# First norm of a layer kernel: raw tiles turned as they land, its weights at the copies from PSUM, its roots at later copies

## The reference, cut to what matters

```python
def rmsnorm(x, g):
    xf = x.astype(jnp.float32)
    y = xf * lax.rsqrt(jnp.mean(xf * xf, axis=-1, keepdims=True) + EPS)
    return (y * g.astype(jnp.float32)).astype(x.dtype)

def layer_forward(x, pos0, lw, pool_prev, rgc_prev, rgh0, sc_prev, nsa_fn):
    h = rmsnorm(x, lw['norm_mix_g'])
    proj = jnp.einsum('bld,dn->bln', h, lw['w_in'])
    pu, rx, rgate, q, kv, ng, sc = split_cols(proj, SPLIT_SIZES)
    ...
    x = x + jnp.einsum('blm,md->bld', y, lw['w_out'])
    x = x + moe_ffn(rmsnorm(x, lw['norm_ffn_g']), ...)
```

## Time and profile before

| | us |
|---|---|
| median of 3 runs | 881.01 |
| lowest, highest | 880.95, 881.67 |
| the profiled execution | 879.65 |
| its span in the trace | 877.9 |
| PE busy, PE weight load | 743.2, 387.7 |
| DVE, ACT, POOL busy | 212.1, 143.0, 188.5 |
| first instruction of PE | 13.67 after the span's start |
| first projection (A0) starts | 20.3 |
| experts begin | about 390 |

### The profile page before, as it was taken

How to read it: one execution, slowest core, us unless ns; L and a number is a source line. 1 busy time by engine, 2 the same in 40 slices (tenths; PEclk the granted TensorE clock), 3 DMA queues, 4 the chain that set the end, 5 groups by cost and what they waited for, 6 DMA issues and landing times.

```text
span 877.9 us, 10180 instructions
## 1 busy us (share of the span) xinstructions
PE 743.2 (85%) x3636; PEld 387.7 (44%) x3636; DVE 212.1 (24%) x571; ACT 143.0 (16%) x348; POOL 188.5 (21%) x188
## 2 busy tenths in 40 slices
PE   3999999979898999949999997878787778777883
PEld 3788788867766645533333332222222222222220
DVE  4231103275849511561011101010010010100110
ACT  4212313104152521110101000000000000000000
POOL 7010000070300000011332331322313213223121
PEclk9999999989987999969999999999999999999997
DMA  9651733020340099249999999999999999999992
GB/s 312 120 150 61 240 132 103 2 74 1 121 168 1 4 395 418 100 160 371 411 411 408 409 410 409 415 406 418 406 416 413 408 412 417 408 416 409 414 416 88
DMA packets 77013, 247.04 MB, mean 281 GB/s; under 512 B 24952, under 2 KB 44303, under 8 KB 52363
## 3 DMA queue, kind: packets, MB, share of 16 engines
q1 hardware_dynamic: 63825, 231.48, 66.8%
q0 software_dynamic: 11776, 8.58, 4.4%
q10 hardware_dynamic: 1378, 6.54, 1.9%
HBM read 240.47 MB, written 24.92 MB: 302 GB/s over the span
## 4 chain that ended last, share of the span: by engine, by line
PE 40%; SPq 32%; DMA 12%; DVE 9%; issue 4%; ACT 2%; POOL 0%; ACTq 0%; POOLq 0%; DVEq 0%
PE bank L1090 36%; SPq L579 22%; SPq L586 10%; DMA reg_b<-in_exp_w_gu 6%; PE bank L1093 3%; DMA reg_a<-in_exp_w_gu 3%; DMA ffn_in<-reg_x 1%; DMA reg_x<-in_x_prompt 1%; DVE reg_a L1758 1%; DVE reg_a L1838 1%; DVE reg_y L2048 1%; DVE reg_a L1748 1%; DVE reg_x L1748 0%; DVE small L1799 0%; ACT reg_y L1073 0%
## 5 line engine op out<-in xcount | busy, mean ns | idle before, releaser
L1090 PE MATMUL bank<-reg_w,reg_y 128*64 128x512 f32 (+2 forms) x512 | 138.5, 586 | 16.9 <-DMA reg_w<-in_exp_w_gu 16.8
L1090 PE MATMUL bank<-reg_a,reg_y 128*64 128x512 f32 x528 | 124.2, 606 | 22.3 <-DMA reg_a<-in_exp_w_gu 16.6
L1090 PE MATMUL bank<-reg_b,reg_y 128*64 128x512 f32 x528 | 122.6, 599 | 20.8 <-DMA reg_b<-in_exp_w_gu 15.1
L2052 DVE TENSOR_TENSOR reg_y<-reg_y,bank 128x256 f32<-128x256 f32 x32 | 13.5, 421 | 418.7 <-ACT reg_y L1073 418.7
L1090 PEld LDWEIGHTS bank<-reg_w,reg_y 128*64 128x64 f32 (+2 forms) x512 | 45.5, 146 | 98.3 <-issue 55.5
L1090 PE MATMUL bank<-reg_b,reg_w 128*128 128x260 f32 x384 | 85.3, 383 | 0.0
L1090 PEld LDWEIGHTS bank<-reg_a,reg_y 128*64 128x64 f32 x528 | 34.7, 138 | 103.2 <-issue 51.1
L1090 PEld LDWEIGHTS bank<-reg_b,reg_y 128*64 128x64 f32 x528 | 34.8, 136 | 99.5 <-issue 56.9
L1090 PEld LDWEIGHTS bank<-reg_b,reg_w 128*128 128x128 f32 x384 | 72.7, 190 | 12.1 <-issue 1.1
L684 POOL TENSOR_TENSOR small<-small 128x1 f32<-128x1 f32 (+4 forms) x18 | 20.4, 1137 | 200.2 <-DVE small L1887 71.2
L754 POOL DMA_INDIRECT out_y_p<-reg_y,reg_h x16 | 25.3, 1582 | 167.2 <-ACT reg_y L1077 167.2
(11 more groups left out here) (340 smaller groups left out, 645.0 us busy)
## 6 DMA issues: line engine op xcount, KB each, us to landing
reg_a<-in_exp_w_gu SPq DMA_DIRECT2D x44, 1024.0 KB, 27.6
reg_b<-in_exp_w_gu SPq DMA_DIRECT2D x44, 1024.0 KB, 28.1
reg_w<-in_exp_w_gu SPq DMA_DIRECT2D x40, 1024.0 KB, 28.0
reg_a<-in_exp_w_down SPq DMA_DIRECT2D x22, 1024.0 KB
reg_b<-in_exp_w_down SPq DMA_DIRECT2D x22, 1024.0 KB, 28.0
reg_h<-in_exp_w_down SPq DMA_DIRECT2D x20, 1024.0 KB
reg_w<-in_w_in SPq DMA_DIRECT2D x9, 1024.0 KB, 10.7
reg_w<-in_w_out SPq DMA_DIRECT2D x2, 2048.0 KB, 10.5
```

What stands on the lines that cost most here:

```text
L1090: return eng.matmul(out, lhsT, rhs, start=start, stop=stop, skip_group_check=True)
L2052: tt(hid[b], silu[b], bank[2 + b][:, 256:512], ALU.mult).then_inc(S["hid_made"], 1)
```

## The change

The weights of the norm are loaded as 8 rows of 128 (4 KB) and turned by PE into `gain_col`, a column per chunk of channels; DVE copies it. PE turns the raw `x_in` tiles, each as soon as its load is there, not `xn`. The copies out of PSUM multiply by `gain_col`: ACT in four activations of 128 columns with a scale for each `xTa`, DVE in one multiply for each `xTb`. ACT's squares stand between these copies. The sample tile still gets its root before it is turned (`xn`, now last in PE's order: bank `xT4`), and its weights at the copy. The roots of tiles 0 to 3 are multiplied in twice: in `kv_rows` as the scale of ACT's copies, which wait for all five roots; and for the features, by a new job `RS`: DVE makes four diagonal matrices from the roots (`root_diag`), PE multiplies them by `ones` after the last projection, so that each partition holds all 512 roots, and DVE multiplies `xnT` (8 x 512 columns) in place by that bank. PE waits for it ahead of `features("U")`. One semaphore of the expert stage is counted on another one, to save a semaphore.

```diff
@@ psum_jobs
-    take("xT4")
+    take("gain")
     for i in range(4):
         take(f"xTa{i}")
         take(f"xTb{i}")
+    take("xT4")
...
+    take("RS")
     take("K3")
     take("R3")
@@ SP
-            eng.dma_start(gain_mix, a["norm_mix_g"].rearrange("l d -> (l d)").partition_broadcast(128)).then_inc(S["gain_loaded"], 16)
+            eng.dma_start(gain_rows, a["norm_mix_g"].rearrange("l (c p) -> (l c) p", p=128)).then_inc(S["gain_loaded"], 16)
@@ ACT
-            for i in TILES:
+            def square_tile(i):
                 eng.wait_ge(x_loaded[i], 16)
                 eng.activation(xn[0:ROWS[i], i, :], x_in[0:ROWS[i], i, :], ACT.Square, accum_out=sumsq[0:ROWS[i], i:i + 1]).then_inc(S["xsq_done"], 1)
-            ps = taken(eng, "xT4")
-            copied(copy(xnT[:, :, SEQ:T], ps[:, 0:64].rearrange("p (c t) -> p c t", c=8)), "xT4")
+            square_tile(4)
+            drained(eng, "gain")
             for i in range(4):
                 ps = taken(eng, f"xTa{i}")
-                copied(copy(xnT[:, 0:4, COL[i]:COL[i] + 128], ps[:, :].rearrange("p (c t) -> p c t", c=4)), f"xTa{i}")
+                for c in range(4):
+                    ins = eng.activation(xnT[:, c, COL[i]:COL[i] + 128], ps[:, 128 * c:128 * c + 128], ACT.Copy, scale=gain_col[:, c:c + 1])
+                copied(ins, f"xTa{i}")
+                square_tile(i)
...
                 ps = taken(eng, f"A{i}")
+                eng.wait_ge(S["rstd_made"], NTILE)
+                root = rstd[0:r, i:i + 1]
...
-                copy(qn_buf[n % 2][0:r, 0:256], ps[0:r, 0:256])
-                copied(copy(rows[0:r, i, 0:256], ps[0:r, 256:512]), f"A{i}")
+                eng.activation(qn_buf[n % 2][0:r, 0:256], ps[0:r, 0:256], ACT.Copy, scale=root)
+                copied(eng.activation(rows[0:r, i, 0:256], ps[0:r, 256:512], ACT.Copy, scale=root), f"A{i}")
...
-                copy(gates[0:r, i, :], ps[0:r, 256:W_LAST])
-                copied(copy(win[0:r, i, :], ps[0:r, 0:256]), f"C{i}")
+                eng.activation(gates[0:r, i, :], ps[0:r, 256:W_LAST], ACT.Copy, scale=root)
+                copied(eng.activation(win[0:r, i, :], ps[0:r, 0:256], ACT.Copy, scale=root), f"C{i}")
@@ PE
+            eng.wait_ge(S["gain_loaded"], 16)
+            filled(turn(claim(eng, "gain")[:, 0:KC], gain_rows), "gain")
+            for i in range(4):
+                eng.wait_ge(x_loaded[i], 16)
+                for k, name in enumerate(("xTa", "xTb")):
+                    ps = claim(eng, f"{name}{i}")
+                    for c in range(4):
+                        ins = turn(ps[:, 128 * c:128 * c + 128], x_in[:, i, 512 * k + 128 * c:512 * k + 128 * c + 128])
+                    filled(ins, f"{name}{i}")
             eng.wait_ge(S["xn_made"], 1)
             ps = claim(eng, "xT4")
...
+            eng.wait_ge(S["root_spread"], 1)
+            ps = claim(eng, "RS")
+            for i in range(4):
+                ins = mm(ps[:, 128 * i:128 * i + 128], ones, root_diag[:, i, :], True, True)
+            filled(ins, "RS")
             turn_qk(4)
...
+            drained(eng, "RS")
             features("U")
@@ DVE
+            def ask_root(n):
+                r = ROWS[TILES[n]]
                 eng.wait_ge(S["xsq_done"], n + 1)
+                ts(sumsq[0:r, TILES[n]:TILES[n] + 1], sumsq[0:r, TILES[n]:TILES[n] + 1], 1.0 / D, EPS, ALU.mult, ALU.add).then_inc(S["rstd_asked"], 1)
+            ps = taken(eng, "gain")
+            copied(eng.tensor_copy(gain_col, ps[:, 0:KC]), "gain")
+            ask_root(0)
+            drained(eng, "gain")
             for i in range(4):
                 ps = taken(eng, f"xTb{i}")
-                copied(eng.tensor_copy(xnT[:, 4:8, COL[i]:COL[i] + 128], ps[:, :].rearrange("p (c t) -> p c t", c=4)), f"xTb{i}")
+                copied(tt(xnT[:, 4:8, COL[i]:COL[i] + 128], ps[:, :].rearrange("p (c t) -> p c t", c=4), gain_col[:, 4:8].unsqueeze(2).to_broadcast([128, 4, 128]), ALU.mult), f"xTb{i}")
+                ask_root(i + 1)
+                if i == 1:
+                    eng.wait_ge(S["rstd_made"], 1)
+                    ts(xn[0:NS, 4, :], x_in[0:NS, 4, :], rstd[0:NS, 4:5], None, ALU.mult).then_inc(S["xn_made"], 1)
+            ps = taken(eng, "xT4")
+            copied(tt(xnT[:, :, SEQ:T], ps[:, 0:64].rearrange("p (c t) -> p c t", c=8), gain_col.unsqueeze(2).to_broadcast([128, KC, NS]), ALU.mult), "xT4")
+            eng.wait_ge(S["rstd_made"], NTILE)
+            for i in range(4):
+                ins = ts(root_diag[:, i, :], ident, rstd[:, i:i + 1], None, ALU.mult)
+            ins.then_inc(S["root_spread"], 1)
...
+            ps = taken(eng, "RS")
+            copied(tt(xnT[:, :, 0:SEQ], xnT[:, :, 0:SEQ], ps[:, :].unsqueeze(1).to_broadcast([128, KC, SEQ]), ALU.mult), "RS")
             eng.wait_ge(S["gates_tanh"], 1)
```

More of the change, by code:

```diff
@@ L214, in layer_kernel @@
         reg_q = Region("reg_q", 2080)
-        small = Region("small", 2399)
+        small = Region("small", 2407)
         gu_w = [r.t[:, 0:8192].rearrange("p (c n) -> p c n", c=8) for r in (reg_a, reg_b, reg_w)]
@@ L234, in layer_kernel @@
         raw = reg_x.t[:, :].rearrange("p (c t) -> p c t", c=2)
-        gain_mix = reg_y.cut(D)
+        gain_rows = reg_y.cut(128)[0:KC]
+        root_diag = reg_y.cut(512, "p (t n) -> p t n", t=4)
         par_rows = reg_y.cut(128)[0:P_ROWS]
@@ L367, in layer_kernel @@
         x1_sq = small.cut(10, "p (t h) -> p t h", t=5)
+        gain_col = small.cut(KC)
         gain_x = small.cut(8, "p (s c) -> p s c", s=2)
@@ L408, in layer_kernel @@
             vcache_loaded consts_made vector_chain pool_chain
[L409 removed]
+            xsq_done rstd_asked rstd_made xn_made root_spread hss_made hrs_made qk_normed gates_tanh gates_raw
             rows_stored states_stored params_made sp_exp_asked sp_exp sample_scores q_masked_made
@@ L810, in kv_rows @@
                     return
-                copy(qn_buf[n % 2][0:r, 0:256], ps[0:r, 0:256])
-                copied(copy(rows[0:r, i, 0:256], ps[0:r, 256:512]), f"A{i}")
+                eng.activation(qn_buf[n % 2][0:r, 0:256], ps[0:r, 0:256], ACT.Copy, scale=root)
+                copied(eng.activation(rows[0:r, i, 0:256], ps[0:r, 256:512], ACT.Copy, scale=root), f"A{i}")
                 ps = taken(eng, f"B{i}")
-                copied(copy(rows[0:r, i, 256:512], ps[0:r, 0:256]), f"B{i}")
+                copied(eng.activation(rows[0:r, i, 256:512], ps[0:r, 0:256], ACT.Copy, scale=root), f"B{i}")
                 ps = taken(eng, f"C{i}")
-                copy(gates[0:r, i, :], ps[0:r, 256:W_LAST])
-                copied(copy(win[0:r, i, :], ps[0:r, 0:256]), f"C{i}")
+                eng.activation(gates[0:r, i, :], ps[0:r, 256:W_LAST], ACT.Copy, scale=root)
+                copied(eng.activation(win[0:r, i, :], ps[0:r, 0:256], ACT.Copy, scale=root), f"C{i}")
             def feature_qk(i):
@@ L1101, in _ @@
             filled(ins, "xT4")
-            for i in range(4):
-                eng.wait_ge(S["xn_made"], i + 2)
-                for k, name in enumerate(("xTa", "xTb")):
-                    ps = claim(eng, f"{name}{i}")
-                    for c in range(4):
-                        ins = turn(ps[:, 128 * c:128 * c + 128], xn[:, i, 512 * k + 128 * c:512 * k + 128 * c + 128])
-                    filled(ins, f"{name}{i}")
             def project_samples():
@@ L1481, in turn_tokens @@
                 eng.wait_ge(x_gathered[b], gathered)
-                eng.sem_inc(S["xe_arrived"], 1)
+                eng.sem_inc(S["gather_asked"], 1)
                 by_channel = xe_rows[b].rearrange("n (p c) -> n c p", c=4)
```

11 lines of the change are left out of this document (1 added, 10 removed).

## The result

The changed kernel takes 874.59 us (median of 5, 871.75 to 875.90) against 881.39 (880.95 to 882.01) of the kernel before in the same comparison: ratio 0.9925, interval 0.991 to 0.994. The profiled execution took 875.42, its span is 873.7 (before: 879.65 and 877.9). The forecast was 876.4, within 874.0 to 878.9: the sign holds, and the time lies in the range, near its lower end. By the medians the gain is 6.8 us where 4.6 was forecast; by the two profiled executions it is 4.2.

The account below looks back on a forecast made before the run. PE's chain from the first projection (A0) was taken to bound the kernel, so A0's gain reaches the end: 7.1 - 0.2 - 0.9 - 1.4 = 4.6 us off the 881.01 median, giving 876.4, range 874.0 to 878.9.

Parts of the forecast that it names:

- The pass: DVE's in-place multiply of 4096 feature columns by the roots in `RS`'s bank: 4.47 us, expected within 4.2 to 4.8.
- The stall: PE waits at sample 7's second half, which gets `RS`'s bank: 4.47 + 0.1 - 3.15 = 1.4 us, bounds 0 and 3.0.
- rival B: At sample 7's second half: DVE's pass ends within its cover, no stall, 1.4 us better, 875.0; chance 0.12.
- rival E: DVE's pass runs at a third of the rate, 13.4 us; PE stands 10.3 and the kernel is slower, 885.3; chance 0.03.
- `RS` on PE: Four matmuls of 128 columns after the last projection, 0.88 us, wholly on the path.
- The gap: PE's wait before tile 0's turned queries: 1.2 us instead of 0.97, as ACT's last copies are scaled; 0.2 lost.
- Rival D: Something not starting with PE sets a later time and swallows the gain, giving 879.5 to 881; chance 0.07.
- the loads: Prompt tiles and weight chunks all land one tile's time, 1.28 us, earlier: tile 0 at 5.85, first chunk at 12.7.
- what A0 waits for: The first projection waits for the sample tile, scaled by 12.55, then small turns; starts at 13.4, 7.1 us earlier.
- Rival C: Before A0: all turns at the clock's low level, rising 2 us into A0; tile 0 1.5 later, 877.9; chance 0.16.
- Roots: POOL's powers, 0.54 us each or 5.10 if held; last at 17.0 or 21.6, ACT needs it at 20.4; no cost.
- The sum: Whole kernel: 7.1 at A0 - 0.2 gap - 0.9 `RS` matmuls - 1.4 stall = 4.6 us gained.

Follow-up runs that it names:

- e4_spread_kept: The changed kernel with the norm weights' 512 KB spread load put back ahead of the prompt tiles, read by nobody; 876.39 us, ratio 0.9956.
- e2_rs_late: The changed kernel with `RS` one stage later: matmuls after sample 7's work, DVE's pass behind the gates' instructions; 873.52 us, ratio 0.9926.
- g1_rs_late: The edit of e2_rs_late to the changed kernel, run once more beside the unedited changed kernel; 875.07 us, ratio 0.9933.
- g2_after: The changed kernel unedited, run as the partner of g1_rs_late; 874.49 us, ratio 0.9938.
- e3_no_rs: The changed kernel without `RS`: no matmuls with ones, no DVE pass, so the features lack their roots; 874.41 us, ratio 0.9935.
- f4_half_first: The changed kernel with `RS` late, the first weight chunk loaded between tiles 1 and 2 and its half of A0 done there; 874.84 us, ratio 0.9935.
- f1_before: The kernel before, unedited, for a second profile and more executions; 879.82 us, ratio 0.9988.
- f2_after: The changed kernel, unedited, run beside a copy of the kernel before; 874.67 us, ratio 0.9923.
- the later pass: The changed kernel with `RS` one stage later, executions of e2_rs_late and g1_rs_late together; 12 executions, median 874.88 us.

## Why the prediction was right, step by step

**What held.** The bound was read right: A0's start carries to the end, through features, attention and experts, less what `RS` costs on the way. *The pass* on DVE took 4.42 us where 4.47 was worked out from two rows of other shapes. (The Trainium skill, VectorE: DVE Perf Modes, in the section on the TRN2 errata, gives (N + 151)/0.96 ns for a float32 `tensor_tensor` add; for 4096 columns that is 4.42, and the trace agrees for this multiply with an operand in PSUM.) *The stall* at sample 7 was 1.41 against 1.4, and doubling the pass lengthened it by the pass. So rival B (no stall) and rival E (13.4 us for the pass) fell. *`RS` on PE* cost 1.00 against 0.9. *The gap* was 1.15 against 1.2. Rival D (swallowed) fell: the first expert load was issued at 301.87 to 303.52 in the four profiles of the changed kernel, against about 302.5 forecast and 307.07 before.

**Mis-sized: the loads.** The step "I move all four tiles and the weight chunks behind them up by one tile's time" moves everything by 1.28 us. By the table at e4_spread_kept no load moved by that. Tiles 0 and 1 came 2.2 us earlier (tile 0 at 5.0, below even my lower bound of 5.3), tiles 2 and 3 and the first chunk only 0.8: the chunk landed at 13.2 where I had 12.7. Why the gain is so uneven no run here shows.

**Wrong: what A0 waits for.** I had the sample tile as the last to come, through tile 1's square, and DVE's scaling at 12.55. In truth ACT's chain was faster: it took up its first copy at 6.26, and each tile took 2.06 us (6.26, 8.32, 10.36, 12.40), not 2.3: a square with its sum gave way to the next copy after 1.04 (7.28 to 8.32), where I had 1.16 and 0.1 more. Its timeline in the changed kernel:

```profile
6.26 1.14 ACT L799 ACTIVATE reg_b<-bank,small 128x128 f32<-128x128 f32 x4 [2.28 <-PE bank L1102]
...
8.32 1.16 ACT L799 ACTIVATE reg_b<-bank,small 128x128 f32<-128x128 f32 x4
```

DVE's timeline there, the sample tile's scaling and the last copy from PSUM:

```profile
10.71 0.74 DVE L1574 TENSOR_SCALAR reg_h<-reg_x,small 8x1024 f32<-8x1024 f32 x1
...
12.68 0.68 DVE L1570 TENSOR_TENSOR reg_b<-bank,small 128x512 f32<-128x512 f32 x1
```

The sample tile was scaled by 11.45 and turned by 12.5. A faster ACT would not have moved it up further, which I had overlooked: its scaling also needs POOL's first root, and POOL made its constants first and began the roots only at 10.10. The scaling starts at 10.71 to 10.74 in every profile but that of e4_spread_kept, whose tiles land later, and in five of them the profile names POOL for the wait (0.17 to 0.27). POOL's timeline in the changed kernel:

```profile
10.10 1.78 POOL L688 TENSOR_TENSOR small<-small 8x1 f32<-8x1 f32 x3 [0.18 <-POOL small L682]
```

Then PE waited 0.85 us more. The profile of the changed kernel names DVE's row L1570 (ending 13.36) for that, but A0 doesn't read what that row writes, tile 3's upper half. The weight chunk landed at 3.4 + 9.8 = 13.2, and in e2_rs_late, g1_rs_late and g2_after the same wait is put down to it (0.99, 0.95 and 1.42 us). Two traces separate the two. In e3_no_rs A0 started at 13.41, before that multiply was over (12.80 + 0.69 = 13.49); in g2_after 0.55 us after it (12.55 + 0.68 against 13.78). The chunk had landed at 13.3 and 13.6. In all ten traces with the norm turned raw, A0's first matmul comes 0.1 to 0.2 us after the first chunk's landing (f4_half_first, which loads it earlier: 11.13 against 11.0). So A0 hangs on the chunk. I had the chunk as the lower bound, 12.7, and the small turns as what sets the time, 13.4; the chunk came 0.5 later than that and the small turns 0.9 earlier, and A0 came at 13.37. The number was right for the wrong reason, and by luck: the order of the two was the other way round. Asking for the chunk earlier, as f4_half_first does it, wins nothing.

**Rival C.** The low level of the clock was there at the start: the first sixteen turns took 3.68 us, 0.22 apart. How long it lasted differed from profile to profile, also among kernels whose program is the same up to there. In g2_after eight turns took 1.09 from 9.23 on, so the upper level was there 4.3 us after PE's first tile turn (4.92). In the changed kernel's own profile the second sixteen turns still took 2.98, and in e3_no_rs all of them ran at the low level, to 12.7, which is 7.9 us after the first (4.79). The moment of the rise thus varied by more than 3 us, not by the 0.5 that C's account quotes. PE's timeline of e3_no_rs:

```profile
9.08 3.68 PE L1101 MATMUL bank<-small,reg_x 128*128 128x128 f32 x16 [0.62 <-DMA reg_x<-in_x_prompt]
...
13.41 14.24 PE L1098 MATMUL bank<-reg_w,reg_b 128*128 128x256 f32 x64
```

So C's condition (all tile turns at the low level) did come up, and it cost nothing there, because the chunk landed only at 13.3. Nor did the wait before A0 cost what C priced. From A0's first matmul to the turns behind its last it took 14.14 us (13.37 to 27.51), and 14.14 in e4_spread_kept too, where PE had not waited (15.31 to 29.45). The kernel before took 14.07 (20.31 to 34.38), not the 13.99 of the chain, which counts from 20.47:

```profile
20.31 14.14 PE L1090 MATMUL bank<-reg_w,reg_b 128*128 128x256 f32 x64
```

**Roots.** POOL's powers took 0.55 each, none was held for 5.1. POOL's timeline, the last two:

```profile
12.85 0.55 POOL L688 TENSOR_TENSOR small<-small 128x1 f32<-128x1 f32 x1 [0.97 <-DVE small L1562]
14.91 0.55 POOL L688 TENSOR_TENSOR small<-small 128x1 f32<-128x1 f32 x1 [1.52 <-DVE small L1562]
```

All are done at 15.5, well before ACT asks for them; the "no cost" held with more room than I gave it.

**The sum.** Forecast 7.1 - 0.2 - 0.9 - 1.4 = 4.6. The trace, from start to start: 6.94 at A0 (20.31 to 13.37; my 7.1 counted from the chain's 20.47), less 0.07 in tile 0's matmuls, 0.19 around the gap (5.90 from 27.51 to 33.41, where it was 5.71), 1.00 for `RS` and 1.60 at the stall (4.51 from sample 7's first turns, 92.36, to the compressed keys, 96.87, where it was 2.91 from 98.11 to 101.02; the profile calls 1.41 of it idle): 4.08. The features start 4.15 earlier. The end is 4.2 earlier in the first pair of profiles and 4.75 by the mean spans.

**What stays open.** The medians give 6.8, 5.9, 5.9 and 5.9 us in the four comparisons (5.2 from f1_before to f2_after), the chain 4.2 to 4.75: about 1 us is not accounted for. Part of the answer is which executions were profiled. The two profiles of the kernel before are of quick ones, 879.65 and 878.89 us, where the median of its 61 executions (f1_before with them) is 880.36; the four of the changed kernel average 874.54, and the median of all 22 is 874.57. That is the missing microsecond, but what the slower executions of before do otherwise no trace shows. From the first expert's result to the end takes 486.9 to 488.6 us in every profile, whichever kernel it is of, and before and after lie on both sides of each other there (488.2, 488.1 against 488.5, 487.1, 488.6, 486.9). The page of the changed kernel, in 40 equal slices, fits a stage bound by its transfers; from the twentieth slice on the weights stream in at 406 to 416 GB/s until the last slice:

```profile
GB/s 299 117 147 73 259 113 95 4 71 1 178 114 0 48 424 352 113 165 399 409 413 410 407 406 414 409 413 416 406 416 413 408 413 414 409 416 410 414 416 83
```

I see no place in it where the change could gain a microsecond, but no run tests it. Executions with a higher mean granted clock tended to be the quicker ones (of the later pass: 869.5 at 0.976, 877.4 at 0.965), which would make the surplus and e3_no_rs's missing gain a matter of that spread. Among the 23 executions of the kernel before in the second comparison this does not show (the slowest, 882.57, at 0.971; the quickest, 878.72, at 0.969). It is an observation, not a shown cause.

## What to carry to other kernels

Follow every item that the first matmul needs, its weights too, each to its own landing time, and keep the second latest as well: the forecast hinged on two that were 0.7 us apart, and they came in the other order. Before adding a long instruction on an idle engine, ask which buffer it holds and who gets that buffer next; the 4.4 us pass had over 20 us of cover and still stalled PE for 1.4, because of the bank's next owner. Two rows of the same kind of instruction priced a new one to 1%. One shift for all the loads behind the one taken out fitted none of them: 2.2 us for the first two and 0.8 for the next three, where I had 1.28. And putting a thing back is not the reverse of taking it out unless all else is as it was: e4_spread_kept gave 2.1 us where the two kernels themselves show 0.8.
